# The grid attention of a two-block transformer: projections by feature, a moved copy, and bias masks made ahead

## The reference, cut to what matters

```python
q, k, v, z = split(u @ in_w, 4)          # latent tokens
_, k_c, v_c, _ = split(uc @ in_w, 4)     # context tokens
# for each query row r; window rows rs.., all 8 rows here; 16 columns allowed
s_loc = q_r @ k_window.T * 64**-0.5 + bias      # relative-position bias by head
s_loc = where(mask, s_loc, -inf)                # a mask of columns only
s_ctx = q_r @ k_c.T * 64**-0.5
p = softmax(concat(s_loc, s_ctx))
o = p_loc @ v_window + p_ctx @ v_c
y = (o * silu(z)) @ out_w;  h = h + gate * y
```

## Time and profile before

| | |
|---|---|
| time, median of 3 runs | 2335.82 us (2335.0 to 2336.82) |
| the profiled execution | 2336.09 us, span 2334.3 us |
| PE, ACT, DVE, POOL busy | 96%, 40%, 56%, 12% of the span |
| chain that ended last | PE 80%, DVE 10%, ACT 5%, issue 3% |
| mean granted clock of PE | 0.994 |

### The profile page before, as it was taken

How to read it: one execution, slowest core, us unless ns; L and a number is a source line. 1 busy time by engine, 2 the same in 40 slices (tenths; PEclk the granted TensorE clock), 3 DMA queues, 4 the chain that set the end, 5 groups by cost and what they waited for, 6 DMA issues and landing times.

```text
span 2334.3 us, 32859 instructions
## 1 busy us (share of the span) xinstructions
PE 2248.6 (96%) x13409; PEld 1859.1 (80%) x13409; DVE 1297.0 (56%) x1890; ACT 925.0 (40%) x1564; POOL 272.2 (12%) x175
## 2 busy tenths in 40 slices
PE   6999999999999999999999999999899999999998
PEld 5876688888888776788888888897787878887777
DVE  4687458963225778369943255216666363126774
ACT  3447742222214357542222232324655242115663
POOL 2001222211002012132211000000000000001220
PEclk9999999999999999999999999999999999999999
DMA  5210035532223210145523321320000224213321
GB/s 157 86 68 2 1 104 182 184 109 90 108 94 94 81 37 2 37 144 171 172 90 108 108 65 51 101 87 13 15 15 15 93 82 141 72 55 75 54 57 55
DMA packets 146088, 191.10 MB, mean 82 GB/s; under 512 B 42229, under 2 KB 95490, under 8 KB 145922
## 3 DMA queue, kind: packets, MB, share of 16 engines
q1 hardware_dynamic: 110288, 169.83, 22.0%
q10 hardware_dynamic: 35586, 19.01, 3.5%
q0 software_dynamic: 64, 0.16, 0.0%
HBM read 181.51 MB, written 7.48 MB: 81 GB/s over the span
## 4 chain that ended last, share of the span: by engine, by line
PE 80%; DVE 10%; ACT 5%; issue 3%; DMA 1%; POOL 1%; ACTq 1%; POOLq 0%; DVEq 0%
PE ps L516 63%; PE ps L1822 3%; PE ps L2391 2%; PE ps L2408 2%; DVE ps L2034 2%; PE ps L2420 2%; DVE probs_t L2064 1%; DVE neg_max L2015 1%; ACT probs L1934 1%; PE ps L1856 1%; PE ps L2396 1%; PE ps L723 1%; DVE sink_part L2023 1%; DVE w_low L481 1%; ACT probs_t L2497 1%
## 5 line engine op out<-in xcount | busy, mean ns | idle before, releaser
L481 DVE TENSOR_TENSOR w_low<-w_raw,w_high 128x2048 fp32r<-128x2048 f32 (+4 forms) x140 | 305.7, 2184 | 497.9 <-ACT w_high L476 497.7
L476 ACT ACTIVATE w_high<-w_raw 128x2048 fp32r<-128x2048 f32 (+4 forms) x140 | 252.9, 1807 | 614.0 <-PE ps L516 603.5
L516 PE MATMUL ps<-h_hi,w_high 128*128 128x512 f32 x976 | 371.7, 381 | 1.6 <-DVE h_lo L2788 0.8
L516 PE MATMUL ps<-h_lo,w_high 128*128 128x512 f32 x976 | 369.1, 378 | 0.0
L516 PE MATMUL ps<-h_hi,w_low 128*128 128x512 f32 x976 | 369.0, 378 | 0.0
L516 PE MATMUL ps<-w_high,h_hi 128*128 128x512 f32 (+3 forms) x736 | 277.4, 377 | 7.8 <-DVE w_low L481 7.1
L516 PE MATMUL ps<-w_low,h_hi 128*128 128x512 f32 (+3 forms) x736 | 274.7, 373 | 0.0
L516 PE MATMUL ps<-w_high,h_lo 128*128 128x512 f32 (+3 forms) x736 | 274.6, 373 | 0.0
L516 PEld LDWEIGHTS ps<-h_hi,w_high 128*128 128x128 f32 x976 | 183.7, 188 | 37.6 <-DVE w_low L481 1.9
L516 PEld LDWEIGHTS ps<-h_hi,w_low 128*128 128x128 f32 x976 | 183.6, 188 | 34.8
L516 PEld LDWEIGHTS ps<-h_lo,w_high 128*128 128x128 f32 x976 | 183.7, 188 | 34.1 <-issue 0.5
(11 more groups left out here) (360 smaller groups left out, 3905.3 us busy)
## 6 DMA issues: line engine op xcount, KB each, us to landing
w_raw<-in_w_gate_up SPq DMA_DIRECT2D x44, 1024.0 KB, 5.1
ada_w<-in_ada_w SPq DMA_DIRECT2D x24, 1024.0 KB, 5.1
w_raw<-in_w_down SPq DMA_DIRECT2D x20, 1024.0 KB, 4.8
w_raw<-in_w_in SPq DMA_DIRECT2D x16, 1024.0 KB, 5.1
w_raw<-in_c_in_w SPq DMA_DIRECT2D x16, 1024.0 KB, 5.6
w_raw<-in_w_out SPq DMA_DIRECT2D x8, 1024.0 KB, 4.8
w_raw<-in_ab_in_w SPq DMA_DIRECT2D x8, 1024.0 KB, 5.1
bias<-bias_scratch ACTq DMA_DIRECT2D x32, 224.0 KB, 4.8
```

Of the source, the lines that this page charges most:

```text
L476: e.activation(w_high[j % 2][:, 0:size], w_raw[j % 2][:, 0:size], ACT.Copy).then_inc(sig.w_high_done, 1)
L481: e.tensor_tensor(w_low[j % 2][:, 0:size], w_raw[j % 2][:, 0:size], w_high[j % 2][:, 0:size].bitcast(F32), ALU.subtract).then_inc(sig.w_lo ...
L516: mm = e.matmul(dst, lhs, rhs, start=start and a == 0, stop=stop and a == 2)
```

## The change

- q and k are projected by feature instead of by token, straight into the layout that the scores read (`q_c`, `k_c` as [P, KD, tokens]); the queries are reversed as they are copied out. The transposes of q and k go, `turns` is empty.
- The high and low parts of a pair are now cut from SBUF in one instruction each (`pair_high` on ACT, `pair_low` on DVE): pair 0 between the k and the v product (`PairAhead`, into buffers of its own), the others in the loop, high parts at iterations 4p - 5 and 4p - 4 and low parts an iteration later.
- DVE's order in the grid stage is new (`grid_iteration`): context maximum, copy of the probabilities, the two bias maxima, then inverse, low part, wide product.
- The spread of the sums (`wide`) comes an iteration later on PE, between turn_probs and values.
- The masks are made during the q and k products: `MaskedBias.beside_load` has SP, behind each of the eight weight pieces, wait for the mask before, store that table in DRAM, wait until the store has landed, and load the next raw table by four DMAs; GpSimd masks it. The last one stays in SBUF for pair 0. In the grid stage one DMA of 896 KB for each pair loads the masked table.
- `BiasAhead` and GpSimd's masks in the loop go, and so do the ten filling matmuls (`keep_warm`) at the grid stage's beginning.

```diff
-        q_c = at("q_c", [P, NT, DM], F32, B1)
-        k_c = at("k_c", [P, NA, DM], F32, B1 + 16384)
+        q_c = at("q_c", [P, KD, S], F32, B1)
+        k_c = at("k_c", [P, KD, ALL], F32, B1 + 16384)
...
-        qc_low = at("qc_low", [P, NT, DM], F32R, B1)
-        kc_low = at("kc_low", [P, NA, DM], F32R, B1 + 16384)
+        qc_low = at("qc_low", [P, KD, S], F32R, B1)
+        kc_low = at("kc_low", [P, KD, ALL], F32R, B1 + 16384)
+        q_first = at("q_first", [P, NT, P], F32R, B1 + 65536)
+        k_first = at("k_first", [P, NA, P], F32R, ROWS_AT)
...
+        masked_dram = nc.dram_tensor("masked_scratch", [CH // 2, P, 2, 14, 64], F32).ap()
...
+                        if self.masks:
+                            self.masks.beside_load(e, B, self.slot + i * self.pieces + j)
...
+                self.cut_at = {4 * p - 5 + c: (p, c) for p in range(1, U) for c in range(2)} if grid else {}
...
-                keep_warm(e, 6, 10 if self.grid else 4)
+                if not self.grid:
+                    keep_warm(e, 6, 4)
...
+                    if self.grid and s - 1 in self.ends:
+                        wide(self.ends[s - 1])
...
-                    if s in self.ends:
+                    if s in self.ends and not self.grid:
                         wide(self.ends[s])
...
                 def load_bias(p):
-                    for m in range(2):
-                        for half in range(2):
-                            e.dma_start(bias2[p % 2][64 * half:64 * half + 64, m, 1:15, :],
-                                        bias_source(2 * p + m, half)).then_inc(sems[f"bias_load{p % 2}"], 16)
+                    e.dma_start(bias2[p % 2][:, :, 1:15, :], masked_dram[p]).then_inc(sems[f"bias_load{p % 2}"], 16)
...
+                    e.wait_ge(sig.bias_stored, B["bias_stored"])
...
+                    if s in self.cut_at:
+                        p, c = self.cut_at[s]
+                        if p >= 2:
+                            e.wait_ge(sig.scores_ready, B["scores_ready"] + 4 * (p - 2) + 4)
+                        pair_high(e, p, c)
...
+                def context_max(s):
+                    two, b = slice(self.col[s], self.col[s + 1]), self.base(s)
+                    e.wait_ge(sig.scores_ready, B["scores_ready"] + s + 1)
                     ch.step(e.tensor_reduce(out=seed2[:, two], in_=flat[:, b + 512:b + 1024].rearrange("p (m n) -> p m n", m=2),
                                             op=ALU.max, axis=AX.X))
+                def grid_max(s, m):
+                    (u, js), b = self.steps[s], self.base(s)
                     j = js[0]
-                    if j == 0:
-                        e.wait_ge(sig.bias_masked, B["bias_masked"] + u)
+                    if j == 0 and m == 0 and u:
+                        name = f"bias_load{u % 2}"
+                        e.wait_ge(sems[name], B[name] + 16 * (u // 2 + u % 2))
+                    elif j == 0 and m == 0:
+                        e.wait_ge(sig.bias_masked, B["bias_masked"])
                     ch.wait(e)
-                    for m in range(2):
-                        a = flat[:, b + 1024 * m:b + 1024 * m + 512]
-                        bias = bias2[u % 2][:, m, 7 - 2 * j:15 - 2 * j, :].rearrange("p r c -> p (r c)")
-                        c = slice(2 * s + m, 2 * s + m + 1)
-                        alone(e)
-                        ch.step(e.tensor_tensor_reduce(a, a, bias, 1.0, seed2[:, c], ALU.add, ALU.max, max2[:, c]))
-                        ch.wait(e)
-                        e.tensor_scalar(neg_max2[:, c], max2[:, c], -1.0, None, ALU.mult).then_inc(sig.max_ready, 1)
+                    a = flat[:, b + 1024 * m:b + 1024 * m + 512]
+                    bias = bias2[u % 2][:, m, 7 - 2 * j:15 - 2 * j, :].rearrange("p r c -> p (r c)")
+                    c = slice(2 * s + m, 2 * s + m + 1)
+                    alone(e)
+                    ch.step(e.tensor_tensor_reduce(a, a, bias, 1.0, seed2[:, c], ALU.add, ALU.max, max2[:, c]))
+                    ch.wait(e)
+                    e.tensor_scalar(neg_max2[:, c], max2[:, c], -1.0, None, ALU.mult).then_inc(sig.max_ready, 1)
...
+                def grid_iteration(s):
+                    if s == self.N:
+                        gate_piece(e, {n: B[n] for n in ("gate_landed", "pair")}, 1, gate_row, 3)
+                    if s + 1 < self.N:
+                        context_max(s + 1)
+                    if 0 <= s < self.N:
+                        copy_probs(s)
+                    if s + 1 < self.N:
+                        grid_max(s + 1, 0)
+                        grid_max(s + 1, 1)
+                    if s in self.ends:
+                        invert(self.ends[s])
+                    if s - 1 in self.cut_at:
+                        p, c = self.cut_at[s - 1]
+                        pair_low(e, B, p, c, 2 * (p - 1) + c + 1)
+                    if s - 1 in self.ends:
+                        gate_wide(self.ends[s - 1])
...
-                else:
-                    e.wait_ge(sig.bias_load1, B["bias_load1"] + 64)
-                    mask_bias(e, 1)
...
-                    p = u + 2
-                    if self.grid and p < self.U:
-                        name = f"bias_load{p % 2}"
-                        e.wait_ge(sems[name], B[name] + 64 * (p // 2 + p % 2))
-                        mask_bias(e, p)
...
-        class BiasAhead(Stage):
-            counts = {"bias_load0": 64, "bias_masked": 1}
-            aside = True
...
+        def pair_highs(p):
+            return (q_first[:], k_first[:]) if p == 0 else (q_high[:, p % 2, 0:NT, :], k_high[:, p % 2, :, :])
+        def pair_parts(p, c):
+            high = pair_highs(p)[c].rearrange("p b c -> p (b c)")
+            return (q_c, k_c)[c][:, p, :], high, (qc_low, kc_low)[c][:, p, :]
+        def pair_high(e, p, c):
+            src, high, _ = pair_parts(p, c)
+            e.activation(high, src, ACT.Copy).then_inc(sig.qk_high, 1)
+        def pair_low(e, B, p, c, n):
+            src, high, low = pair_parts(p, c)
+            e.wait_ge(sig.qk_high, B["qk_high"] + n)
+            e.tensor_tensor(low, src, high.bitcast(F32), ALU.subtract).then_inc(sig.qk_ready, 1)
+        class PairAhead(Stage):
+            counts = {"qk_high": 2, "qk_ready": 2}
+            aside = joined = True
 
             def scalar(self, e, B, L, ch):
-                for m in range(2):
-                    for half in range(2):
-                        e.dma_start(bias2[0][64 * half:64 * half + 64, m, 1:15, :], bias_source(m, half)).then_inc(sig.bias_load0, 16)
+                e.wait_ge(sig.evac_act, B["evac_act"])
+                e.wait_ge(sig.evac_vec, B["evac_vec"])
+                for par in range(2):
+                    e.wait_ge(sems[f"z_store{par}"], B[f"z_store{par}"])
+                for c in range(2):
+                    pair_high(e, 0, c)
+            def vector(self, e, B, L, ch):
+                for c in range(2):
+                    pair_low(e, B, 0, c, c + 1)
+        class MaskedBias(Stage):
+            counts = {"bias_raw": 64 * (CH // 2), "bias_masked": CH // 2, "bias_stored": 16 * (CH // 2 - 1)}
+            aside = joined = True
+            order = (1, 2, 3, 4, 5, 6, 7, 0)
+            table = bias2[0][:, :, 1:15, :]
 
             def gpsimd(self, e, B, L, ch):
-                e.wait_ge(sig.bias_load0, B["bias_load0"] + 64)
-                mask_bias(e, 0)
+                mask = cst("colmask").unsqueeze(1).unsqueeze(1).to_broadcast([P, 2, 14, 64])
+                for n in range(len(self.order)):
+                    e.wait_ge(sig.bias_raw, B["bias_raw"] + 64 * (n + 1))
+                    e.tensor_tensor(self.table, self.table, mask, ALU.add).then_inc(sig.bias_masked, 1)
+            def beside_load(self, e, B, n):
+                before = lambda name: B[name] - self.counts[name]
+                if n == 0:
+                    e.wait_ge(sig.part_low, B["part_low"])
+                elif n < len(self.order):
+                    e.wait_ge(sig.bias_masked, before("bias_masked") + n)
+                    e.dma_start(masked_dram[self.order[n - 1]], self.table).then_inc(sig.bias_stored, 16)
+                    e.wait_ge(sig.bias_stored, before("bias_stored") + 16 * n)
+                if n < len(self.order):
+                    for m in range(2):
+                        for half in range(2):
+                            e.dma_start(bias2[0][64 * half:64 * half + 64, m, 1:15, :],
+                                        bias_source(2 * self.order[n] + m, half)).then_inc(sig.bias_raw, 16)
...
-            BiasAhead(), GateIn(),
-            from_in("tok", 0, 512, CopyOut(lambda i, m, t0: q_c[:, m, ds(i * 512, 512)], HD ** -0.5), w="c_in_w_2", groups=2, joined=True),
-            from_in("tok", DM, 512, CopyOut(lambda i, m, t0: k_c[:, m, ds(i * 512, 512)]), w="c_in_w_2", groups=2, tokens=ALL, joined=True),
+            masked_bias, GateIn(),
```

(59 more changed lines are left out.)

41 lines of the change are left out of this document (18 added, 23 removed).

## The result

The changed kernel takes 2321.89 us, median of 4 runs (2320.52 to 2322.26); the kernel before took 2335.7 beside it. The ratio is 0.9941, 95% interval 0.9928 to 0.9953: 13.8 us faster, where 18.8 were forecast. The profiled execution took 2321.64 with a span of 2319.8, so 14.5 less than the span of before.

The account below looks back on a forecast made before the run. DVE's order, its copy behind two operations the next scores don't need, was taken to bound the grid stage. From 2336.09: -17.4 - 4.9 + 0.1 + 1.6 - 0.9 + 2.5 = -19.0, less 0.27 for the median, 2317; range 2311 to 2327.

Parts of the forecast that it names:

- rival A: Whole kernel: the time comes out as the terms were summed, 2317, own range 2312 to 2322; chance 0.60.
- Grid step: Grid stage: with the copy moved forward a step takes 4.45 us instead of 5.09, gaining 17.4 over 27 steps.
- rival C: Products and grid stage: no collision of mask and weight cut, and steps at PE's floor, 2313; chance 0.09.
- rivals B: Grid stage: the step stays near 4.75 because an exponential or unit-end operation is late, 8 more, 2325; chance 0.20.
- D: Grid stage: the loop isn't cut and steps keep 5.01, some 2326 to 2329; chance 0.04.
- Start of the stage: Way into the grid stage: exponential 0 comes 3.0 us sooner and scores 4 come 4.9 sooner; the tail loses 0.1.
- Products: Products ahead of the grid stage: keys by feature +1.6, queries 0, PE's wait behind ACT's bias loads gone, -0.9.
- The first mask meets a weight cut: z product: GpSimd's first mask, starting at 1919 to 1922, may hold w_low and PE; +2.5 taken, up to 5.
- SP's queue: q and k products: a slot of load, mask and store takes 15.6 us; first value piece early by 8.7, no stall.
- Rival E: SP's lane: weight pieces arrive late behind mask, store and load; 2322 at a 17.9 slot, 2331 at 19.4; chance 0.07.
- sign of 5 us or more: SP's queue: a store of 5 us or more was listed as showing the forecast wrong; 3.5 was taken.
- The sum of 2322: Products: total if a w_low that came first also held the mask, as the page says; 2317 by the rows.

Follow-up runs that it names:

- run 4: Changed kernel with DVE's old order in the grid stage, the copy of the probabilities behind both bias maxima again: 2341.17 us, ratio 1.0021.
- run 5: Kernel before with one edit, DVE's copy of the probabilities put between the context maximum and the bias maxima in the grid stage: 2326.41 us, ratio 0.9962.
- run 6: Changed kernel with the spread of the sums (wide) back in its old place on PE, behind values: 2330.28 us, ratio 0.9979.
- Run 1: Changed kernel with every mask slot one weight piece later: 2312.67 us, ratio to the kernel before 0.9907.
- run 3: Changed kernel with 32 filling matmuls on PE between z's third and last weight piece: 2321.33 us, ratio 0.9942.
- runs 2: Changed kernel, but GpSimd's first mask waits until DVE has made z's last lower part (w_low): 2316.59 us, ratio 0.9925.
- run 9: Changed kernel with one more GpSimd mask of each pair's table in the loop, loads still one DMA a pair: 2338.02 us, ratio 1.0015.
- run 7: Changed kernel with biases loaded raw by four ACT loads a pair and masked by GpSimd in the loop, as before the change: 2334.51 us, ratio 0.9993.
- run 8: Changed kernel with each pair's masked table loaded by four DMAs of 224 KB instead of one, no mask in the loop: 2318.37 us, ratio 0.9938.

## Why the prediction was right, and where it was short

The forecast was 2317, the measured time 2321.89. The grid stage came out by the mechanism given; the products came out 5.1 longer than forecast (8.3 over before, where the sum had 3.2), and z's start added 1.2. That the time still lies in rival A's own range, 2312 to 2322, and by 0.1 us only, is luck: the steps gained 1.9 more than the sum had.

**Grid step: right, a little small.** 4.45 was forecast, 4.38 measured: -19.3 against -17.4. The step of 4.27 from the earlier trace rows is 4.26. The spread costs 0.44, not 0.6, and none of the operations that I had at 0 to 0.15 us of slack came late: PE waits for nothing in 125 us. Runs 4 to 6 show that the loop went for the reason given: the copy put back (run 4) brings the old loop back, the copy moved alone (run 5) gives PE's own steps but for kc_low's hold, and `wide` put back (run 6) brings a wait on DVE's inverse. The time would have been that of rival C in this stage; rivals B and D are out.

**Start of the stage: right.** Scores 4 come 4.9 sooner after v_c, the first exponential 3.1 sooner (3.0 forecast). The tail's 0.1 is 0.1.

**Products: +0.7 forecast.** Run 1, where PE waits for nothing in them, has +0.4.

**The first mask meets a weight cut: the step that was mis-sized.** Forecast +2.5 with bounds 0 and 5; it cost 5.2 and, behind it, 2.8 that no term had. The collision was the whole of a mask, not the middle: the mask started 0.33 ahead of w_low. The estimate of its start, 1919 to 1922, was too early, because the four loads took 1924.83 - 1912.59 = 12.24 and not 7.77; SP alone needed 8.25 to issue them while the weight piece ahead was landing. The same loads stretched the z store to 6.32 (4.6 before), which moved w_low from 1922.26 to 1925.16. Both came 2.9 or so later than the rows had them, 1.2 of it from z's own start, and they met. The term that I left out is the clock: I priced the wait and not what a PE that stands still for 5 us gets granted next. Run 1 returns both; run 3 returns the clock, though only 1.1 of its 2.8 reach the time.

**SP's queue: the slot was right, the point of measurement wrong.** Starts of the masks lie 15.7 to 16.7 apart from the second on (15.6 forecast), the 896 KB store lands in 4.0 (3.5 taken), and PE waits on no w_low in the k product. The first slot was longer, 22.6: its store, issued just behind a weight piece, took 7.8, so one store did show the sign of 5 us or more. And the margin was worked out for v's first piece alone (8.7; measured 5.3: its lower part ready at 2050.3, PE there at 2055.6). At k's first it is 1.3, and only because the lower clock has already delayed PE; in runs 2, 3, 4, 6 and 9 it is gone, and PE waits 1.4 to 2.5. Rival E was nearer than its chance, also in its mechanism: in four of these runs a running w_low did hold a mask back.

**What the prediction did not see at all.** It costed the masks' leaving the loop at ACT's and SP's queues only. Their worth is elsewhere: the change makes the lower parts from SBUF instead of PSUM, and such a cut stands still for as long as GpSimd's mask runs. With masks in the loop the new kernel would be at 2334.5 (run 7) to 2338 (run 9), so moving them ahead is worth at least 12.6 us to it. The row for it was there (w_low at 5.08 beside a mask), and I used it for the first mask only. The Trainium skill ("SBUF — State Buffer", Who interferes with whom) has the rule that parts the two: a DVE instruction with two SBUF inputs contends with a GpSimd instruction that reads SBUF, one with at most one, outside the 2-port modes, does not. The runs agree: 3.85 against 0.95 for the cut with both operands in SBUF, at most 0.68 for the one from PSUM (its second operand is in SBUF). The page's sentence that whoever issues first has the pair for the whole instruction agrees for a mask that comes first (run 9's kept its 4.02), and, what no row of before showed, for a cut that comes first. Ahead of the grid stage of run 9, DVE's timeline:

```profile
1945.46 2.29 DVE L487 TENSOR_TENSOR w_low<-w_raw,w_high 128x2048 fp32r<-128x2048 f32 x1 [13.68 <-ACT w_high L482]
```

and POOL's:

```profile
1946.50 5.18 POOL L2225 TENSOR_TENSOR bias<-bias,con 128x1792 f32<-128x1792 f32 x1 [19.07 <-DMA bias<-bias_scratch]
```

w_low keeps its 2.29 and the mask ends 3.93 after it, a mask's own length. The sum of 2322 that I gave to that order was the measured time, but by another way: in the changed kernel the mask came first.

**Open.** In the changed kernel and its versions z's second piece starts anywhere from 1899.95 to 1904.86, with the same code ahead of it; up to 4.9 us between single profiles is that. It goes with the granted clock between 1550 and 1800: 0.97 in the five profiles that start at 1903.44 or later, 0.98 in the three from 1900.86 to 1902.08, 0.99 in run 8. Why the clock differs there is not shown. And run 1 still has masks that meet a w_low, hidden by the weight buffers; whether a slot later still would bring more was not tried.

## What to carry to other kernels

Where a vector engine sets the pace without being full, look for the one output that another engine waits for and put it ahead of what nobody waits for yet; here one copy was worth 19 us, but only 9 in the old loop, where TensorE's own transposes and, less so, the lower key part then set the step. What moves behind others by it (here the inverse) needs a later consumer, or 9 us go again. Before an operation's source is moved from PSUM to SBUF, see what GpSimd does at that time. And when a wait on TensorE is priced, price the clock behind it, and work out a queue's margin at the first consumer it can reach, not only at the last.

## What the runs showed of the hardware

- A DVE subtraction with both inputs in SBUF did nothing while a GpSimd mask of 4.0 us ran: 3.85 for 0.95 (768 columns), 5.81 and 5.59 for 2.30 (2048 columns). Where the subtraction came first, the mask was held: 5.18 in run 9, 6.10 in run 4.
- After 5.3 us without matmuls the granted clock was 0.73 for the next 11 us (1.00 with filling matmuls in the gap). Runs 4, 8, 6 and 9, with gaps of 5.1, 4.8, 4.8 and 4.1 us at the same place, show 0.77, 0.77, 0.86 and 0.85.
- Four DMAs of 224 KB in rows of 256 bytes took SP 8.25 us to issue behind a weight piece, where ACT had issued such four in 3.34, and 3.01 later in the same kernel.
- 896 KB out of SBUF landed in 4.0 us (7.8 once, just behind a weight piece), 512 KB in 2.6.
